# A fused attention and feed-forward layer: two of eight row blocks of the first feed-forward product by a seven-product scheme

## The reference, cut to what matters

```
x = x + nsa_mixer(rms_norm(x, g_mix), ...)
h = rms_norm(x, g_mlp) @ w1             # 256 x 2048 by 2048 x 8192
x = x + square(relu(h)) @ w2            # 256 x 8192 by 8192 x 2048
x = x + sigmoid(rms_norm(x, g_ple) @ w_gate) * (p @ w_proj)
```

## Time and profile before

| | |
|---|---|
| median of 3 runs | 1196.61 us (1196.56 to 1197.06) |
| the profiled execution: time on the device | 1196.38 us |
| its span, first to last instruction | 1194.6 us |
| PE busy | 1188.6 us (99%) |
| DVE busy | 735.8 us (62%) |
| ACT busy | 591.0 us (49%) |
| POOL busy | 72.1 us (6%) |

### The profile page before, as it was taken

One profiled execution on the slowest core, in us unless ns is written; L12 is line 12 of the kernel. 1 busy time (PEld: TensorE's weight loads), 2 busy tenths in 40 slices (PEclk: granted clock), 3 DMA queues, 4 the chain that ended last, 5 costly groups with the idle time before them and its releaser, 6 DMA issues.

```text
span 1194.6 us, 14118 instructions
## 1 busy us (share of the span) xinstructions
PE 1188.6 (99%) x5468; PEld 988.8 (83%) x5468; DVE 735.8 (62%) x977; ACT 591.0 (49%) x808; POOL 72.1 (6%) x63
## 2 busy tenths in 40 slices
PE   9999999999999999999999999999999999999998
PEld 7888888888888888888888888888888888888886
DVE  6568867878776565554555655556555566476554
ACT  6745555666655544433444433445433454455443
POOL 1000100000000011100011100012000011000000
PEclk9999999999999999999999999999999999999999
DMA  9858673333368567765577766676755677786661
GB/s 347 318 168 249 205 255 118 110 118 124 106 184 299 184 205 256 237 215 194 190 228 256 230 203 194 193 252 222 248 193 194 213 236 224 242 265 196 222 201 50
DMA packets 110979, 249.25 MB, mean 209 GB/s; under 512 B 9664, under 2 KB 55744, under 8 KB 110912
## 3 DMA queue, kind: packets, MB, share of 16 engines
q1 hardware_dynamic: 110768, 248.34, 64.0%
q10 hardware_dynamic: 144, 0.01, 0.0%
HBM read 233.63 MB, written 14.68 MB: 208 GB/s over the span
## 4 chain that ended last, share of the span: by engine, by line
PE 99%; DMA 0%; DVE 0%; SPq 0%; ACT 0%; issue 0%
PE acc L1510 91%; PE sc L1653 1%; PE sc L1618 1%; PE tr L1570 1%; PE tr L1559 0%; PE sc L1559 0%; PE tr L1706 0%; PE tr L1705 0%; PE acc L1542 0%; PE tr L1682 0%; DMA w_raw<-in_nsa_w_in_units_dram 0%; PE tr L1688 0%; PE tr L1683 0%; PE tr L1668 0%; PE tr L1666 0%; PE tr L1708 0%
## 5 line engine op out<-in xcount | busy, mean ns | idle before, releaser
L1010 DVE TENSOR_TENSOR w_split<-w_raw,w_split 128x1024 fp32r<-128x1024 f32 x408 | 506.2, 1249 | 377.6 <-ACT w_split L645 376.9
L645 ACT ACTIVATE w_split<-w_raw 128x1024 fp32r<-128x1024 f32 x408 | 428.3, 1058 | 410.1 <-PE acc L1510 404.3
L1510 PE MATMUL acc<-w_split,a_hi 128*128 128x512 f32 x1916 | 594.2, 392 | 0.2 <-DVE w_split L1006 0.2
L1510 PE MATMUL acc<-w_split,b_split 128*128 128x512 f32 x1920 | 441.0, 390 | 0.0
L1510 PEld LDWEIGHTS acc<-w_split,b_split 128*128 128x128 f32 x1920 | 359.4, 188 | 73.9
L1510 PEld LDWEIGHTS acc<-w_split,a_hi 128*128 128x128 f32 x1916 | 356.8, 188 | 74.1 <-issue 1.1
L1510 PE MATMUL acc<-w_split,a_lo 128*128 128x512 f32 x958 | 373.6, 390 | 0.0
L1510 PEld LDWEIGHTS acc<-w_split,a_lo 128*128 128x128 f32 x958 | 179.9, 188 | 37.8
L604 POOL TENSOR_TENSOR stage<-stage 128x512 f32<-128x512 f32 x32 | 49.6, 1568 | 559.3 <-ACT stage L653 559.3
L747 ACT ACTIVATE s<-s,nmx,q_scale 128x128 f32<-128x128 f32 (+1 forms) x64 | 34.2, 538 | 10.2 <-DVE nmx L1188 10.2
L653 ACT ACTIVATE stage<-acc,rstd 128x512 f32<-128x512 f32 x48 | 30.1, 679 | 11.0 <-PE acc L1510 9.5
(11 more groups left out here) (184 smaller groups left out, 517.6 us busy)
## 6 DMA issues: line engine op xcount, KB each, us to landing
w_raw<-in_mlp_w_units_dram SPq DMA_DIRECT2D x256, 512.0 KB, 4.4
w_raw<-in_nsa_w_in_units_dram SPq DMA_DIRECT2D x76, 512.0 KB, 4.7
w_raw<-in_nsa_w_out_units_dram SPq DMA_DIRECT2D x32, 512.0 KB, 4.4
w_raw<-in_ple_w_gate_units_dram SPq DMA_DIRECT2D x32, 512.0 KB, 4.2
turn_dram<-s SPq DMA_DIRECT2D x52, 128.0 KB, 4.1
turn_dram<-junk SPq DMA_DIRECT2D x44, 128.0 KB, 4.0
v_slc<-turn_dram SPq DMA_DIRECT2D x22, 256.0 KB, 4.0
v_win<-turn_dram SPq DMA_DIRECT2D x22, 256.0 KB, 4.1
```

The source lines that it names most:

```text
L645: nc.scalar.activation(w_hi[:, u % SPLIT], w_raw[:, u % RAW], ACT.Copy).then_inc(hi_done, 1)
L1010: nc.vector.tensor_tensor(w_lo[:, u % SPLIT], w_raw[:, u % RAW], f32(w_hi[:, u % SPLIT]), ALU.subtract).then_inc(lo_done, 1)
L1510: last = nc.tensor.matmul(acc[c % 2][t][:], xs[:, kt, toks], ws[:, u % SPLIT, m * NW:(m + 1) * NW], start=(kt == 0 and n == 0), stop=(kt = ...
```

## The change

The 16 chunks of the first product, but for the first two, are now made two at a time as *pairs* (7 pairs). In a pair, PE goes through the 8 row blocks of 256 rows and multiplies each with 1024 columns. For row blocks 4 and 6 (`QUADS`) the 2 x 2 by 2 x 2 block product is made by the Winograd form of Strassen's scheme: 7 block products in place of 8, four of them with combinations of weight blocks (made by DVE in the raw places, then split by ACT and DVE into `t_hi`, `t_lo`) and four with combinations of activation blocks (made once, `combined_rows`, in `r_hi`, `r_lo`). Three products go straight into an output's bank; four sums (`mixes`) have banks of their own, so that a pair uses all eight banks, and are combined by ACT and DVE in an SBUF tile `mixed` (`keep_one`, `mix`) and added to the outputs' banks (`pair_sums`). ReLU and squaring of the pairs' outputs are both done by ACT (`hidden_out`); POOL squares no more. The weight places `w_split` of a quad are given back after its first nine matmuls.

In the second product three chunks run side by side, half of their units at a time (`down_order`; the third sums in `sc`), then the fourth alone. The SP loads follow, without the extra `i` arguments, and the turns go with them. In the last quarter `turn_back` and `turned_gain` of set `T_H2 + 1` come later. Several SBUF tiles are laid out anew, so that the new ones lie over those of the attention.

`combined_rows` (DVE, after units 5 and 6 of chunk `C_MLP + 1`) makes six small operations, and ACT rounds their result after unit 7.

```diff
+PAIR_NO = {C_MLP + 8 * q + 2 * p: 2 * q + p - 1 for q in range(QUARTERS) for p in range(2) if q or p}
+QUADS = (4, 6)
+N_QUADS = len(QUADS)
...
+def raw_free(u):
+    return u + 2 if u in QUAD_UNITS else u + 1
...
+def down_order():
+    halves = range(UPC // 2), range(UPC // 2, UPC)
+    return [(n, k) for half in halves for n in range(3) for k in half]
...
+        def pair_banks(c):
+            if PAIR_NO[c] == 0:
+                return tr + sc, mlp_acc[0] + mlp_acc[1]
+            if (c - C_MLP) % 8 == 0:
+                return mlp_acc[0] + sc, tr + mlp_acc[1]
+            return tr + mlp_acc[1], mlp_acc[0] + sc
...
-                if not (isinstance(i, int) and u < RAW):
-                    sp.wait_ge(lo_done, u - RAW + 1 + i)
+                if u >= RAW:
+                    sp.wait_ge(lo_done, raw_free(u - RAW))
...
+            def hidden_turns(n, s, first):
+                if s == first:
+                    turn_away(n)
+                if s == first + 2:
+                    turn_back(n)
+                    turn_away(n + 1)
...
+            def down(q):
+                c, n = C_MLP + 8 * q + 4, T_HID + 4 * q
+                for s, (m, k) in enumerate(down_order()):
+                    if s == 0 and q:
+                        turn_back(n + 1)
+                    load(FIRST[c] + s, packed(w2_units, m, UPC * q + k), slot(FIRST[c] + s))
+                    hidden_turns(n + 2, s, 12)
+                    if s == 16:
+                        turn_back(n + 3)
...
-            def square(c, i=0):
-                for t in range(TT):
-                    pool.wait_ge(acc_read[c % 2][t], c // 2 + 1 + 4 * i)
-                    nc.gpsimd.tensor_tensor(stage[:, t], stage[:, t], stage[:, t], ALU.mult)\
-                      .then_inc(squared, 1)
-            for q in range(QUARTERS):
-                for j in range(4):
-                    square(C_MLP + j, q)
...
+            def split_hi_pair(c):
+                for s in range(2 * UPC):
+                    u = FIRST[c] + s
+                    act.wait_ge(raw_full[u % RAW], 16 * (u // RAW + 1))
+                    act.wait_ge(unit_used, u - SPLIT + 1)
+                    if u - 1 not in QUAD_UNITS:
+                        nc.scalar.activation(w_hi[:, u % SPLIT], w_raw[:, u % RAW], ACT.Copy).then_inc(hi_done, 1)
+                        yield s
+                        continue
+                    at = QUAD_UNITS.index(u - 1)
+                    nc.scalar.activation(w_hi[:, u % SPLIT, NW:UW], w_raw[:, u % RAW, NW:UW],
+                                         ACT.Copy).then_inc(hi_done, 1)
+                    if at:
+                        act.wait_ge(quad_used, at)
+                    for half, v in enumerate((u, u - 1)):
+                        act.wait_ge(sums, 2 * at + half + 1)
+                        nc.scalar.activation(t_hi[:, half], w_raw[:, v % RAW], ACT.Copy).then_inc(sums_hi, 1)
+                    yield s
...
+            def keep_one(c):
+                n, mixes = PAIR_NO[c], pair_banks(c)[1]
+                act.wait_ge(quad_used, N_QUADS * (n + 1))
+                nc.scalar.activation(mixed[:, 0], mixes[0][:], ACT.Copy).then_inc(one_copied, 1)
+            def hidden_out(c, half):
+                n = PAIR_NO[c]
+                t_set = T_HID + (c - C_MLP) // 8 * 4 + (c - C_MLP) % 8 + half
+                act.wait_ge(blocks_turned, TT * t_set)
+                for t in range(TT):
+                    src = mixed[:, 2 * half + t]
+                    act.wait_ge(summed, 4 * n + 2 * half + t + 1)
+                    nc.scalar.activation(src, src, ACT.Relu, scale=rstd[:, 1, t:t + 1]).then_inc(relu_done, 1)
+                for t in range(TT):
+                    act.wait_ge(relu_done, 4 * n + 2 * half + t + 1)
+                    nc.scalar.activation(stage[:, t], mixed[:, 2 * half + t], ACT.Square).then_inc(squared, 1)
...
+                for s in split_hi_pair(c):
+                    if s == 2 * UPC - 1:
+                        keep_one(c)
+                    if p and q:
+                        if s in (3, 5):
+                            hidden_out(c - 2, s // 2 - 1)
...
+            def split_lo_pair(c):
+                for s in range(2 * UPC):
+                    u = FIRST[c] + s
+                    dve.wait_ge(hi_done, u + 1)
+                    if u in QUAD_UNITS:
+                        nc.vector.tensor_tensor(w_lo[:, u % SPLIT], w_raw[:, u % RAW],
+                                                f32(w_hi[:, u % SPLIT]), ALU.subtract)
+                        continue
+                    if u - 1 not in QUAD_UNITS:
+                        nc.vector.tensor_tensor(w_lo[:, u % SPLIT], w_raw[:, u % RAW],
+                                                f32(w_hi[:, u % SPLIT]), ALU.subtract).then_inc(lo_done, 1)
+                        yield s
+                        continue
+                    at = QUAD_UNITS.index(u - 1)
+                    nc.vector.tensor_tensor(w_lo[:, u % SPLIT, NW:UW], w_raw[:, u % RAW, NW:UW],
+                                            f32(w_hi[:, u % SPLIT, NW:UW]), ALU.subtract).then_inc(direct, 1)
+                    b11, b21 = (w_raw[:, (u - 1) % RAW, m * NW:(m + 1) * NW] for m in range(2))
+                    b12, b22 = (w_raw[:, u % RAW, m * NW:(m + 1) * NW] for m in range(2))
+                    dve.wait_ge(direct, at + 1)
+                    nc.vector.tensor_tensor(b11, b11, b12, ALU.add).then_inc(first_sums, 1)
+                    dve.wait_ge(first_sums, 2 * at + 1)
+                    nc.vector.tensor_tensor(b12, b12, b22, ALU.add).then_inc(first_sums, 1)
+                    dve.wait_ge(first_sums, 2 * at + 2)
+                    nc.vector.tensor_tensor(b22, b11, b22, ALU.add).then_inc(sums, 1)
+                    dve.wait_ge(sums, 2 * at + 1)
+                    nc.vector.tensor_tensor(b21, b22, b21, ALU.add).then_inc(sums, 1)
+                    for half, v in enumerate((u, u - 1)):
+                        dve.wait_ge(sums_hi, 2 * at + half + 1)
+                        nc.vector.tensor_tensor(t_lo[:, half], w_raw[:, v % RAW], f32(t_hi[:, half]),
+                                                ALU.subtract).then_inc(lo_done, 1)
+                    yield s
...
+            def mix(c):
+                n, (_, five, six, seven) = PAIR_NO[c], pair_banks(c)[1]
+                dve.wait_ge(one_copied, n + 1)
+                if n:
+                    dve.wait_ge(squared, 2 * TT + 4 * n)
+                nc.vector.tensor_tensor(mixed[:, 3], six[:], mixed[:, 0], ALU.subtract).then_inc(mix_step, 1)
+                dve.wait_ge(mix_step, 2 * n + 1)
+                nc.vector.tensor_tensor(mixed[:, 2], five[:], mixed[:, 3], ALU.add)
+                nc.vector.tensor_tensor(mixed[:, 1], seven[:], mixed[:, 3], ALU.add).then_inc(mix_step, 1)
+                dve.wait_ge(mix_step, 2 * n + 2)
+                nc.vector.tensor_tensor(mixed[:, 3], five[:], mixed[:, 1], ALU.add).then_inc(mix_ready, 1)
+            def pair_sums(c):
+                n, (c11, c21, c12, c22) = PAIR_NO[c], pair_banks(c)[0]
+                dve.wait_ge(unit_used, END[c])
+                dve.wait_ge(mix_ready, n + 1)
+                for m, bank in enumerate((c11, c21, c12)):
+                    nc.vector.tensor_tensor(mixed[:, m], bank[:], mixed[:, m], ALU.add).then_inc(summed, 1)
+                nc.vector.tensor_tensor(mixed[:, 3], c22[:], mixed[:, 3], ALU.subtract).then_inc(summed, 1)
...
+                for s in split_lo_pair(c):
+                    if s == 2 * UPC - 1:
+                        mix(c)
...
+                    if not p and s == 2:
+                        add_to_h(c - 1, 3)
+                    if p and q:
+                        if s == 2:
+                            pair_sums(c - 2)
+                        if s in (4, 6):
+                            turn_hidden(n + s // 2 - 2)
+                        if s == 14:
+                            turned_hidden(0, q)
...
+            def down_pair(q):
+                c, n = C_MLP + 8 * q + 2, T_HID + 4 * q + 2
+                for s in split_lo(FIRST[c + 2], 2 * UPC):
+                    if s == 0 and q:
+                        turned_hidden(1, q)
+                    if s == 2:
+                        pair_sums(c)
+                    if s in (4, 6):
+                        turn_hidden(n + s // 2 - 2)
+                    if s in (11, 14):
+                        turned_hidden(s // 3 - 1, q)
...
-                if k == 6:
+            for k in split_lo(FIRST[C_PLE], UPC + 1):
+                if k == 0:
                     turned_gain(T_H2 + 1, a_hi, a_lo, 4, GAIN_PLE)
-            for k in split_lo(FIRST[C_PLE], UPC + 1):
...
+            def quad(c, i, banks, mixes):
+                n, k = PAIR_NO[c], QUADS[i]
+                u, at = FIRST[c] + 2 * k, N_QUADS * n + i
+                def split(x, v, m):
+                    return tuple(y[:, v, m * NW:(m + 1) * NW] for y in x)
+                def combined(r):
```

(79 more changed lines are left out.)

309 lines of the change are left out of this document (189 added, 120 removed).

## The result

The changed kernel takes 1187.68 us (median of 4 runs, 1187.33 to 1187.91), the kernel before 1196.84 us in the same comparison (1196.56 to 1197.06). The ratio is 0.9923, 95% interval 0.9906 to 0.9941: 0.77% faster. The forecast was 1187.8 us, its range 1186.5 to 1191.5. The profiled execution took 1187.8 us, its span is 1186.1 us.

The account below looks back on a forecast made before the run. PE was taken as the bound, busy for 99% of the span. 1196.4 - 9.5 (42 fewer matmuls) + 0.7 (late first quads) = 1187.6 us; the median stands 0.2 above, 1187.8, range 1186.5 to 1191.5.

Parts of the forecast that it names:

- The sum: Whole kernel: 1196.4 us less 9.5 for 42 fewer matmuls, plus 0.7 of waits: 1187.6, median 1187.8 us.
- The line of steps of a quad: ACT and DVE steps ending in the split of the sums; a pair's first quad late by 0 to 0.3 us.
- S: The time at which PE begins row block 4, the first quad of a pair.
- 0.1 a quad: Lateness taken for the first quad of each pair: 7 x 0.1 = 0.7 us, bounds 0 and 2.1.
- The second quad: DVE's last split ends near S + 11.7, wanted at S + 12.24: late by nothing, spare 0.2 to 0.3 us.
- The seam: Between two pairs PE waits for the mixes to be copied and combined; fits by 0.2 us, cost 0.
- rival 3: DVE becomes the bound if a quad's additions and splits take 2.06 us, not 1.22: 34 us lost, 1221; chance 0.04.
- rival 4: PE's clock falls to 1.2 GHz for one unit after each first quad: 18 us, 1206; chance 0.02.
- The argument from the earlier trace: Against rival 4: PE paused about half a microsecond (0.57) at the trace's start, and the clock still read nine tenths or more.

Follow-up runs that it names:

- the extra step: The changed kernel with the DVE subtraction of half a unit in each quad made twice, the second waiting for the first: 1194.88 us.
- the two extra steps: The changed kernel with the first of the four operations that combine the mixes made three times, each waiting for the last: 1194.69 us.
- ReLU and turns spread: Against three quads in all 7 pairs (7 raw places): in second pairs, ACT's second ReLU lot after unit 9, DVE's turns after units 6 and 10; 1196.24 us.

## Why the prediction was right

- **The sum.** 42 matmuls at 0.2267 us: 9.52 counted; removing just that saving costs 9.7 (9.53 between the marks). Lost inside: 0.7 counted, 0.62 in the trace, and 0.60 back when the sums are made early. 1187.8 forecast, 1187.68 measured.
- **The line of steps of a quad.** Its end was counted at S + 1.87 and stands at S + 1.84 once, at S + 1.90 or 1.91 five times and at S + 2.18 once. An estimate to 0.04 us over ten steps, in six quads of seven, was possible because each had a row of its own form in the trace of before, waits among them: 0.73 for an operation that waits, 0.61 for one that doesn't. The rule of the Trainium skill ("VectorE: DVE Perf Modes", The DRAIN you can't avoid), by which a semaphore costs nothing here, would have had the sums ready 0.4 us earlier and nothing lost; the additions of the changed kernel start 0.73 apart, and the trace disagrees with it again. With that much room the extra step could have cost no more than 0.73 - 0.4 = 0.3 us in a first quad.
- **Where it was luck.** I spread the loss evenly, 0.1 a quad. It is 0.02 to 0.05 in six quads and 0.3 in the one at 934 us, whose late start of ACT no step of the count foresaw. Without that one the loss would have been 0.3 us, so that 0.62 agrees with 0.7 is in part luck. The choice of 0.1 in the range from 0 to 0.3 was not worked out either. A wait that is this close to its limit shows the small shifts of everything ahead of it.
- **The second quad.** Its terms as printed add up to S + 12.5 and not S + 11.7; they give 11.7 only if the wait for ACT is counted from the end of the third addition, beside the fourth, and that is how it went: S + 11.6, and no loss. DVE as a whole was put at 835 us and came to 813.8, so its load was taken too high, on the safe side.
- **The seam.** 0.2 us of spare was counted, 0.4 is what the two extra steps found. The copy of a bank took 0.60 where 0.68 was taken.
- **DVE as the bound** (rival 3) did not come: 36.4 of 42.2 us, and no split of weights or sums over 1.23 us. With three quads in a pair PE does stand, though with 40.5 us of DVE work beside 41.5 of its own; DVE's total is not the bound there either, the hand-overs between DVE and ACT come first.
- **The clock** (rival 4) stayed at 2.4 GHz behind waits of 0.1 to 0.5 us of the weight loads in the changed kernel, and behind longer ones in the one with the extra step (0.8 and 1.2 us by PE and by its weight loads; all slices read nine tenths or more). In the two versions with three quads everywhere it fell behind two of three pauses of 2.81 us and two of four of 1.9. So a fall behind a pause of PE does happen, but for longer pauses than this change makes. The argument from the earlier trace rows was read wrongly: 0.57 us is the idle time of the weight loads there, PE's own was 0.17, so that row said little about pauses of half a microsecond. The page of the Trainium skill on the clock ("TensorE: Matmul & The Clock Gate", HAM oscillation) names waits for data between batches of matmuls as what makes it fall; these runs agree in kind.
- **Open.** Why half a unit was rounded 0.3 us later in quarter 3 was not tried. In all quads but the very first ACT also begins to round the sums 0.09 us behind the third addition, where it is 0.03 in the first; the code waits for one more semaphore there (`quad_used`), but that this is the reason was not tried. What the layout of SBUF alone does was not tried either, only that everything beside the matmuls together is worth a few hundredths of a microsecond.

## What to carry to other kernels

When one engine is the bound for 99% of the time, cutting its instructions paid in full here as long as the helpers' longest *dependent line* fitted between the moment a place comes free and the moment it is wanted. Busy shares (69% of DVE) don't say whether it does; a count step by step from rows of the same form does, with the waits in it. Nor does the total of a stretch: with three quads DVE had 40.5 us of work in 41.5, and PE stood for 3.7 us and more. Look for steps in that line which don't need what they wait for: two additions on raw data, made earlier, took the loss away and made room for more quads where DVE had time. And place more of a good thing stage by stage: three quads in the pairs with idle DVE gave all of their 2 us, with the crowded pairs among them the kernel lost 14 us against two quads.

## What the runs showed of the hardware

- Behind a pause of PE of 2.81 us the granted clock was at 0.50 for about 7 us, and a matmul of 512 columns took 0.43 us in place of 0.227. The same pause in the same trace was followed by 3.4 us at 0.50 at another place and by none at a third. Of four pauses of 1.9 us (three with ReLU and turns spread, one at 990 us without) two were followed by 3.4 us at 0.50 and two by none. The length of the pause alone does not say what the clock does. In the kernel whose pauses reach 0.8 us (1.2 by the weight loads) no slice reads under nine tenths.
- Runs of one kernel with such pauses (three quads, ReLU and turns spread) differ in time as their granted clocks do: 1193.7 to 1195.0 us at a mean granted clock of 0.999 or more, 1196.1 to 1198.4 at 0.996 to 0.998.
- DVE operations with two SBUF operands take up to 2.06 us for 128 x 1024 (1.22 else) while POOL squares; one that takes PSUM and SBUF stays at 0.68 us for 128 x 512.
- PE loses a few hundredths to a tenth of a microsecond in the matmuls behind a late weight load, besides the wait: 0.19 of wait, 0.12 of restart in the quad at 934 us, and 0.11 in each of the 14 quads of the kernel with the extra step.
